# Gate rows made by four transposes of the copied gate columns, behind the transposes of k and v

## The reference, cut to what matters

```python
g = -jnp.exp(a_log) * jax.nn.softplus(a + dt_bias)      # one gate per frame and head
G = jnp.cumsum(gc, axis=-1)                              # cumulated within the chunk
decay = jnp.exp(jnp.where(causal, G[..., :, None] - G[..., None, :], -jnp.inf))
lower = jnp.where(strict, jnp.einsum('bhnid,bhnjd->bhnij', k_beta, kc) * decay, 0.0)
rhs = jnp.concatenate([v_beta, k_beta * jnp.exp(G)[..., None]], axis=-1)
k_tail = kc * jnp.exp(G[..., -1:] - G)[..., None]
g_last = jnp.exp(G[..., -1])
```

## Time and profile before

| | us |
|---|---|
| median of 3 runs | 2315.89 (2314.6 to 2316.67) |
| the profiled execution, its own time | 2316.02 |
| its span, first to last instruction | 2314.2 |
| PE busy | 2194.2 (95%) |
| DVE busy | 1675.6 (72%) |
| ACT busy | 782.7 (34%) |
| POOL busy | 652.4 (28%) |

### The profile page before, as it was taken

The page is one execution under the profiler, slowest core; times in us unless marked ns, Lnnn a source line. Parts: engine busy times, 40 slices in busy tenths (PEclk is TensorE's granted clock), DMA queues, the critical chain, the costliest instruction groups (busy, mean ns, idle before and its releaser), DMA issues.

```text
span 2314.2 us, 61174 instructions
## 1 busy us (share of the span) xinstructions
PE 2194.2 (95%) x25926; PEld 1887.4 (82%) x25926; DVE 1675.6 (72%) x4495; ACT 782.7 (34%) x2008; POOL 652.4 (28%) x875
## 2 busy tenths in 40 slices
PE   0389999999999999999999999999999999999996
PEld 0378888888888888888888888888888888888874
DVE  5887767777777777777777777677777777777774
ACT  0533333333333333333333333333333333333332
POOL 0022323232232332232323223232322323322322
PEclk9999999999999999999999999999999999999998
DMA  7100000000000000000000000000000000000000
GB/s 296 50 21 30 25 7 30 30 30 30 30 6 25 30 30 30 30 30 2 30 30 30 30 30 22 10 30 30 30 30 30 4 28 30 30 30 30 21 1 28
DMA packets 26321, 75.19 MB, mean 32 GB/s; under 512 B 5129, under 2 KB 9538, under 8 KB 25026
## 3 DMA queue, kind: packets, MB, share of 16 engines
q1 hardware_dynamic: 26050, 71.29, 8.9%
HBM read 54.50 MB, written 16.78 MB: 31 GB/s over the span
## 4 chain that ended last, share of the span: by engine, by line
PE 93%; DVE 4%; DMA 1%; ACT 1%; issue 0%; SPq 0%; POOLq 0%; POOL 0%; DVEq 0%; ACTq 0%
PE bank L402 36%; PE bank L594 14%; PE bank L409 11%; PE bank L417 9%; PE bank L432 4%; PE bank L452 3%; PE bank L528 2%; PE bank L562 2%; PE bank L436 2%; DVE w_raw L1204 1%; PE bank L549 1%; PE bank L380 1%; PE bank L471 1%; PE bank L440 1%; PE bank L457 1%; PE bank L444 1%
## 5 line engine op out<-in xcount | busy, mean ns | idle before, releaser
L402 PE MATMUL bank<-xt_half,w_raw 128*128 128x128 f16 x15360 | 931.2, 219 | 54.8 <-DVE w_raw L1204 54.3
L402 PEld LDWEIGHTS bank<-xt_half,w_raw 128*128 128x128 f16 x15360 | 893.9, 98 | 62.3 <-DVE w_raw L1204 54.5
L867 DVE SCALAR_TENSOR_TENSOR qkv<-conv_in,cols,qkv 128x128 f32<-128x128 f32 x1152 | 431.4, 417 | 3.5
L409 PE MATMUL bank<-w_raw,xt_half 128*128 128x264 f16 (+1 forms) x1536 | 283.0, 328 | 0.0
L1261 POOL TENSOR_TENSOR cw<-mt,small 128x256 f32<-128x256 f32 x160 | 114.7, 725 | 409.8 <-PE bank L432 388.6
L409 PEld LDWEIGHTS bank<-w_raw,xt_half 128*128 128x128 f16 x1536 | 147.9, 98 | 77.7 <-issue 5.3
L694 ACT ACTIVATE work<-bank 128x256 f32<-128x256 f32 x160 | 61.3, 383 | 430.9 <-PE bank L436 430.9
L594 PE MATMUL bank<-w_o,inv_t 128*128 128x512 f16 x768 | 171.0, 379 | 2.1 <-DVE inv_t L1140 2.1
L594 PE MATMUL bank<-w_o,out_b_half 128*128 128x512 f16 x768 | 171.0, 379 | 0.0
L659 ACT ACTIVATE tanh_c<-qkv 128x512 f32<-128x512 f32 x96 | 60.5, 630 | 270.2 <-DVE qkv L867 270.2
L594 PEld LDWEIGHTS bank<-w_o,inv_t 128*128 128x128 f16 x768 | 73.8, 98 | 85.4 <-DVE inv_t L1140 2.4
(11 more groups left out here) (219 smaller groups left out, 3878.5 us busy)
## 6 DMA issues: line engine op xcount, KB each, us to landing
x_in<-in_x_dram SPq DMA_DIRECT2D x32, 512.0 KB, 4.4
y_out<-in_x_dram SPq DMA_DIRECT2D x32, 512.0 KB, 3.9
out_dram<-y_out SPq DMA_DIRECT2D x32, 512.0 KB, 2.9
w_raw<-in_w_in_dram SPq DMA_DIRECT2D x8, 1024.0 KB, 12.4
w_o<-in_w_out_dram SPq DMA_DIRECT2D x8, 512.0 KB, 13.1
w_raw<-in_w_in_dram SPq DMA_DIRECT2D x8, 384.0 KB, 11.6
w_raw<-in_w_in_dram SPq DMA_DIRECT2D x8, 256.0 KB, 12.4
rot_tab<-in_rotary_dram SPq DMA_DIRECT2D x32, 64.0 KB, 4.0
```

Source lines behind the costliest of these rows:

```text
L402: last = mm(dst[:, 128 * b:128 * b + 128], w_half[:, c, ws, col:col + 128], xt_half[:, xs, c, :], start=(c == 0 and ws + xs == 0), stop=(c ...
L409: last = mm(dst[:, 0:n_col], xt_half[:, xs, c, :], w_half[:, c, ws, col:col + n_col], start=(c == 0 and ws + xs == 0), stop=(c == NC - 1 a ...
L867: last = v.scalar_tensor_tensor(dst, conv_in[:, b, i:i + TOK], tap, dst, ALU.mult, ALU.add)
```

## The change

The four cumulating matmuls of line 471 go. In their place, four transposes of the copied columns (each column of `g_cols` broadcast to 128 columns) give the same rows in bank 2. They stand behind the transposes of v, ahead of `fill(3)`, and wait for `g_cols_used`, DVE's copy of the columns. That wait stood ahead of the transposes of q before, and leaves there. On DVE the copy of the columns comes first, and the copy of the last values behind it, with a semaphore of its own, `g_last_ready`.

```diff
                 done(pe, g_ready, m)
-                done(pe, state_ready, m - 1)
-                for h in range(4):
-                    last = mm(bank[2][:, 128 * h:128 * h + 128], g_tok[:, h:h + 1].broadcast_to([128, 128]),
-                              upper, start=True, stop=True)
-                last.then_inc(g_row_t, 1)
                 done(pe, out_a_ready, m - 1)
                 mm(bank[3][:, 0:4], upper, g_tok, start=True, stop=True).then_inc(g_col_t, 1)
...
                 last.then_inc(v_turned, 1)
+                done(pe, g_cols_used, m)
+                done(pe, state_ready, m - 1)
+                for h in range(4):
+                    last = nc.tensor.transpose(heads(2)[:, h, :], g_cols[:, h:h + 1].broadcast_to([128, 128]), ident)
+                last.then_inc(g_row_t, 1)
                 fill(3)
...
                 per_head(5, k4, q4, gram_t)
-                done(pe, g_cols_used, m)
                 for h in range(4):
                     last = nc.tensor.transpose(heads(3)[:, h, :], q4[:, h, :], ident)
...
+                    done(dve, g_col_t, m)
+                    done(dve, exp_cols_ready, m - 1)
+                    v.tensor_copy(g_cols[:, 0:4], bank[3][:, 0:4]).then_inc(g_cols_used, 1)
                     done(dve, g_row_t, m)
-                    done(dve, exp_cols_ready, m - 1)
-                    v.tensor_copy(g_cols[:, 8:12], heads(2)[:, :, TOK - 1])
-                    done(dve, g_col_t, m)
-                    v.tensor_copy(g_cols[:, 0:4], bank[3][:, 0:4]).then_inc(g_cols_used, 1)
-                    done(dve, g_cols_used, m)
+                    v.tensor_copy(g_cols[:, 8:12], heads(2)[:, :, TOK - 1]).then_inc(g_last_ready, 1)
+                    done(dve, g_last_ready, m)
                     v.tensor_tensor(g_cols[:, 4:8], g_cols[:, 8:12], g_cols[:, 0:4], ALU.subtract)
```

More of the change, by code:

```diff
@@ L222, in build @@
             sem(n) for n in ("gram_t", "k_turned", "v_turned", "q_turned", "sq_ready"))
-        norm_link, k_norms_ready, norms_ready, key_norm_ready, m_ready, at_ready, vn_ready, k_tail_ready = (
-            sem(n) for n in ("norm_link", "k_norms_ready", "norms_ready", "key_norm_ready", "m_ready", "at_ready",
+        norm_link, g_last_ready, k_norms_ready, norms_ready, key_norm_ready, m_ready, at_ready, vn_ready, k_tail_ready = (
+            sem(n) for n in ("norm_link", "g_last_ready", "k_norms_ready", "norms_ready", "key_norm_ready", "m_ready", "at_ready",
                              "vn_ready", "k_tail_ready"))
```

## The result

| | before | after |
|---|---|---|
| median | 2315.89 us | 2344.63 us (4 runs, 2342.06 to 2347.79) |
| ratio | | 1.0127, 95% interval 1.0111 to 1.0142 |
| the profiled execution, its own time | 2316.02 us | 2342.5 us |
| its span | 2314.2 us | 2340.7 us |
| period of a tile | 68.09 us | 68.77 us |

A forecast was written before the change was run, and what follows sets the result against it. PE was taken to bound the kernel. 21.0 us (tiles 1 to 30), 7.7 (tile 0) and 0.5 (tile 31) make 29.2 on the profiled 2316.02; from the median, 2345 us was forecast, range 2337 to 2359, chance 0.84.

The forecast's parts named there:

- PE bounds, and a us on PE is a us: From tile 1 to 30 PE never stands still, so each us of its work or new idle time counts fully.
- Removed 0.88, added 0.43 us: On PE, line 471's instructions go (0.88 us a tile) and four transposes come (0.43); without waiting, 0.45 gained a tile.
- The far end of the bound: If the broadcast transposes take line 471's 0.88 us, `fill(3)` starts 1.15 us later in a tile.
- The wait: Behind v's transposes PE waits 1.08 us for DVE's column copy; `fill(3)` starts 0.70 us later a tile.
- the signs named in advance: In the later trace: column-copy wait 32 times, 36 us in all; period 0.70 longer; PE busy some 14 us less.
- What comes behind: DVE's line 1154 starts 0.52 us later, its cover before the Gram products grows to 1.09 us; no cost, tiles 1-30.
- Tile 0: In the first tile PE stops 8.8 us for the copy, then about 3 us of low clock: +7.7 us.
- Tile 31: In the last tile DVE's line 1154 starts later: +0.5 us, with 3 us up or down for the low clock.
- The clock in every tile: Rival: the new PE stop lets the clock fall in each tile, 46 us more, 2391 us; chance 0.05.
- That the stop shrinks to what line 471 gives back: Rival: PE's stop is only 0.45 us a tile, giving 2324, or no change without tile 0's loss; chance 0.04.
- That the copy comes in time: Rival: DVE's column copy lands before PE needs it, tiles 1 to 31 gain 0.45 us each, 2310; chance 0.03.
- A second wait in every tile: Rival: Gram products wait for `y_used` on DVE's late decay arguments; 0.5 us a tile would give 2360; chance 0.04.

The follow-up runs named there:

- the early-copy version: The changed kernel with DVE's copy of the gate columns moved ahead of the silu of q; 2304.63 us, ratio 0.9943.
- behind `fill(1)`: The changed kernel with the column wait and four transposes behind the first of three projection pieces, DVE's order unchanged; 2320.65 us, ratio 1.0013.
- the version with tile 0 in the old form: The changed kernel, but the first tile makes its rows by the old matmuls; in other tiles PE's two waits change places; 2337.3 us, ratio 1.0088.

## Why the prediction was right, point by point

The mechanism and the size of the wait were right. That the median came within 0.4 us of the 2345 is luck: it is the middle between two pairs of runs some 5 us apart, and in the profiled execution tile 0 (+0.5 against the forecast), the start (+1.1), tiles 1 to 30 (-0.6) and tile 31 (-3.7) missed in both directions.

- **PE bounds, and a us on PE is a us.** Right. In the kernel before 0.61 us more of DVE cost nothing, and in the early-copy version 0.44 us less of PE gave 0.46 us.
- **Removed 0.88, added 0.43 us.** Right: the transposes without a stop in front take 0.44 (279.50 to 279.94). The far end of the bound, two passes for a broadcast operand, is out.
- **The wait.** The step that decided, and right in place and size: 0.68 us a tile against 0.70. The release took 0.06 (copy ends 1182.69, transposes start 1182.75) and the transposes 0.49 with the restart, both as worked out; of the 0.02, 0.01 is DVE's copy, which came after 7.10 us and not 7.11, and the rest is rounding. The wait was sized at 0.9 by the records and showed 0.92; its total was put at 36 and is 36.9. One of the signs named in advance failed: PE's busy time was to fall by some 14 us and fell by 9.0. In a steady tile it fell by 0.24 us (68.09 to 68.77 less the 0.92 of idle time) and not by 0.45, since the transposes take 0.49 behind the stop, and the last 0.17 us of v's transposes (0.60 long, where the next group could have started after 0.43), which overlapped other work before, count as busy now.
- **What comes behind.** Right: in the changed kernel line 1153 ends at 1186.16, 1.10 us ahead of the Gram products; 1.09 was forecast. When the rows came 0.44 us later still (behind `fill(1)`), that cover was gone.
- **Tile 0.** Forecast 7.7, measured 8.2. The stop was 8.59 as against 8.8 in the prediction, where it was counted without the overlap of matmul ends; what was mis-sized is the low clock behind it: I took 3 us and it lasted about 4 (0.50 from 149 to 153), so `fill(3)` took 5.54 and not 5.10.
- **Tile 31.** Forecast +0.5, in the profiled execution -3.2, inside the 3 us and a little. The mechanism gave its 0.5: line 1153 started at once behind line 967 and not at POOL's release. The rest is clock. Of the forecast this is the term that rows of one execution can't give, and it is why the forecast of 2345.2 for the profiled execution missed its 2342.5 by more than the median.
- **The rivals.** The clock in every tile: out. Over 1000 us in the middle, PE stood idle 12.9 us in 14.5 stops, and the granted clock stayed full:

```profile
1000.00:2000.00 1000.00, 987.09 (x11731) 846.95 (x11730) 722.20 (x2011) 340.42 (x901) 298.12 (x395) 1.00 0.07 25
```

 The Trainium skill's rule ("TensorE: Matmul & The Clock Gate", "A second HAM failure mode: psum-queue depth-cycling") that frequent short gaps make the clock swing is not borne out by these rows for one gap of 0.92 us in 68.77; with the DVE instruction added the gaps were 1.53 us, and the granted clock over the same 1000 us was 1.00 too. Tile 31, with its many gaps of 0.3 to 2.8 us between short groups, does what that section describes: after the change its granted clock went from 1.00 to 0.50 and back twice within 20 us. That the stop shrinks to what line 471 gives back: out, it was 1.09 us from where PE could have started (6.22) to where it did (7.31), with 1.08 forecast. That the copy comes in time: out for the change, and reached by moving it; the early-copy version is that rival made true, with 2304.6 and not the 2310 that I had given it, since there tile 0 loses less too (75.03 us for its stretch, +1.8, because the copy comes ahead of the output weights as well). A second wait in every tile: not in the change, but 0.30 us of it in the version behind `fill(1)`.

## What to carry to other kernels

Before an operand is taken from another engine's copy, find the point from which both engines' paths start and add up each to where they meet: here 6.2 against 7.3 us, and the 0.45 us that the cheaper instruction saves was spent two and a half times over (1.09 for the stop, 0.05 for the start behind it). Then look for idle time of the producer ahead of the meeting point and put the small copy there; an engine that waits 0.7 us for someone else in every tile has room for a 0.15 us copy. And look at the first and the last tile by themselves: the cover that the steady tiles have is missing there.

## What was not expected of the hardware

The last stretch, with nearly the same work, took from 65.9 to 73.0 us in eleven profiles, as the granted clock over 54 us of it went from 0.94 to 0.75, and 136 unused matmuls in it brought five runs within 0.8 us of each other. In the version with tile 0 in the old form the stop in the other tiles was 1.01 us and not 0.92:

```profile
279.14 0.15 DVE L965 COPY small<-bank 128x4 f32<-128x4 f32 x1
279.44 0.62 PE L488 MATMUL bank<-c,small 128*128 128x128 f32 x4 [1.01 <-DVE small L965]
```

The transposes started 0.15 us behind the end of the copy instead of 0.06, and so in all thirty tiles from 1 to 30 (0.15 or 0.16, against 0.06 or 0.07 in the changed kernel). In these tiles the two programs differ in one thing, the order of PE's two waits: here the wait for `state_ready` comes first and the one for the copy, which is the late one, last; in the changed kernel the late one comes first. That this order is the cause is not shown, since no run changed it alone.
